# High and low parts side by side: one weight load for 512 columns in the FFN and short-convolution layers of a two-block float32 kernel

## The reference, cut to what matters

```python
def conv_ffn(h, w_up, w_conv, b_conv, w_down):          # twice; D_FF = 2816
    u = h @ w_up                                        # 1024 -> 2 * 2816
    u = depthwise_conv3(u, w_conv) + b_conv             # along the sequence
    val, gate = jnp.split(u, 2, axis=-1)
    return (jax.nn.silu(gate) * val) @ w_down           # 2816 -> 1024

def shortconv_mixer(h, w_in, conv_w, w_out):            # once; WIDTH = 1536
    u = jnp.einsum('bsd,dc->bsc', h, w_in)              # 1024 -> 4 * 1536
    bg, cg, xv, gate = split into four
    y = bg * causal_depthwise_conv(cg * xv, conv_w)
    return jnp.einsum('bsc,cd->bsd', y * jax.nn.silu(gate), w_out)
```

## Time and profile before

| | |
|---|---|
| time, median of 3 runs | 920.02 us (919.19 to 920.58) |
| the profiled execution's own time | 921.24 us |
| its span | 919.5 us |
| mean granted TensorE clock | 0.985 |
| TensorE busy | 881.4 us (96%) |
| VectorE busy | 630.4 us (69%) |
| ScalarE busy | 504.2 us (55%) |
| bytes read from HBM | 151.14 MB, 166 GB/s over the span |

### The profile page before, as it was taken

One profiled execution on the slowest core, in us unless ns is written; L12 is line 12 of the kernel. 1 busy time (PEld: TensorE's weight loads), 2 busy tenths in 40 slices (PEclk: granted clock), 3 DMA queues, 4 the chain that ended last, 5 costly groups with the idle time before them and its releaser, 6 DMA issues.

```text
span 919.5 us, 15132 instructions
## 1 busy us (share of the span) xinstructions
PE 881.4 (96%) x5832; PEld 806.4 (88%) x5832; DVE 630.4 (69%) x848; ACT 504.2 (55%) x676; POOL 34.3 (4%) x76
## 2 busy tenths in 40 slices
PE   7999989999999998899999999999999899999996
PEld 7977769999999876678999999979999699999995
DVE  6798757777666678766776766757877665554643
ACT  6754545455555463545645545558988664353431
POOL 2000100000000023101000000000000000000001
PEclk9999999999999999799999999999999999999998
DMA  9453632745445424054464454516353035545521
GB/s 340 148 200 127 223 137 96 269 143 225 183 149 220 179 95 180 0 185 166 179 240 169 186 205 157 211 65 229 135 231 139 23 138 207 213 162 197 171 81 46
DMA packets 22443, 152.80 MB, mean 166 GB/s; under 512 B 2528, under 2 KB 2656, under 8 KB 5120
## 3 DMA queue, kind: packets, MB, share of 16 engines
q1 hardware_dynamic: 22032, 149.71, 44.1%
q0 software_dynamic: 368, 2.49, 0.7%
HBM read 151.14 MB, written 1.05 MB: 166 GB/s over the span
## 4 chain that ended last, share of the span: by engine, by line
PE 81%; DVE 7%; ACT 5%; issue 1%; POOL 1%; POOLq 0%; ACTq 0%; DVEq 0%
PE ring L1335 47%; PE acc L1348 24%; PE ring L1313 2%; DVE w_lo L761 2%; PE acc L1515 1%; PE ring L1600 1%; PE acc L1280 1%; PE ring L1319 1%; PE ring L1551 1%; ACT xn L457 1%; PE acc L1575 1%; ACT w_hi L448 1%; DVE x L814 0%; ACT pm L647 0%; DVE cacc L1018 0%
## 5 line engine op out<-in xcount | busy, mean ns | idle before, releaser
L761 DVE TENSOR_TENSOR w_lo<-raw,w_hi 128x2048 fp32r<-128x2048 f32 (+1 forms) x146 | 317.8, 2199 | 101.1 <-ACT w_hi L448 100.9
L1335 PE MATMUL ring<-h_hi,w_hi 128*128 128x256 f32 x1264 | 358.6, 284 | 0.0
L1335 PE MATMUL ring<-h_hi,w_lo 128*128 128x256 f32 x1264 | 357.7, 283 | 0.0
L1335 PE MATMUL ring<-h_lo,w_hi 128*128 128x256 f32 x1264 | 357.6, 283 | 0.0
L448 ACT ACTIVATE w_hi<-raw 128x2048 fp32r<-128x2048 f32 (+1 forms) x146 | 264.3, 1839 | 25.4 <-DMA raw<-in_stream_dram 21.8
L1335 PEld LDWEIGHTS ring<-h_lo,w_hi 128*128 128x128 f32 x1264 | 240.7, 190 | 1.5
L1335 PEld LDWEIGHTS ring<-h_hi,w_hi 128*128 128x128 f32 x1264 | 240.7, 190 | 1.4
L1335 PEld LDWEIGHTS ring<-h_hi,w_lo 128*128 128x128 f32 x1264 | 240.7, 190 | 0.0
L1018 DVE SCALAR_TENSOR_TENSOR cacc<-ring,par,cacc 128x255 f32<-128x255 f32 x176 | 76.8, 478 | 52.2 <-ACT cacc L575 47.1
L1348 PE MATMUL acc<-w_hi,a_hi 128*128 128x512 f32 x272 | 107.7, 396 | 3.9 <-DVE a_lo L1195 2.6
L1348 PE MATMUL acc<-w_hi,a_lo 128*128 128x512 f32 x272 | 107.6, 396 | 0.0
(11 more groups left out here) (211 smaller groups left out, 890.8 us busy)
## 6 DMA issues: line engine op xcount, KB each, us to landing
raw<-in_stream_dram SPq DMA_DIRECT2D x134, 1024.0 KB, 4.8
raw<-in_stream_dram SPq DMA_DIRECT2D x12, 512.0 KB, 5.0
gatew<-in_gatew_dram POOLq DMA_DIRECT2D x1, 1536.0 KB, 6.8
x<-in_x_dram SPq DMA_DIRECT2D x2, 512.0 KB, 3.8
out_dram<-xn SPq DMA_DIRECT2D x2, 512.0 KB, 2.6
row<-in_row_dram POOLq DMA_DIRECT2D x1, 640.0 KB, 9.7
gup_raw<-in_gup_dram SPq DMA_DIRECT2D x3, 128.0 KB, 7.0
par<-in_par_dram SPq DMA_DIRECT2D x1, 274.0 KB, 4.5
```

What stands on the lines that cost most here:

```text
L761: nc.vector.tensor_tensor(w_lo[:, u % RING, 0:n], raw[:, u % RAW, 0:n], w_hi[:, u % RING, 0:n].bitcast(f32), ALU.subtract).then_inc(lo_spl ...
L1335: last = nc.tensor.matmul(ring[:, b, f * S:(f + 1) * S], w_parts[a][:, slot, lo:lo + P], h_parts[c][:, kc, :], start=kc == 0 and n == 0, s ...
```

## The change

`h_hi` and `h_lo` become two views of one tile `hh`, high and low side by side for each kc, so that `hh[:, kc, :, :]` is 512 columns. A new function `merged` computes an up unit: for each f and kc one product of `w_hi` by the 512 columns and one of `w_lo` by the 256 high columns, 32 products with 32 loads in place of 48 with 48. The high-by-high and low-by-high sum stands in the left half of a bank, the high-by-low sum in the right half, so a unit now takes two banks (k = 0: banks 0 and 1, k = 1: banks 2 and 3). ACT copies the right halves into a new tile `usum` (`crossed`), DVE adds the left halves to it (`summing`), and all that read the bank before now reads `usum`. TensorE waits for `summed` in place of `ring_free`.

The first unit of each layer goes through `first_merged` (48 products of 256 columns as before, but into two banks), and the last up unit of each of the three layers stays with `wide`, in bank 2 alone, without `usum`. The splits of coming units stand elsewhere in the steps of ACT and DVE.

```diff
-        h_hi = put("h_hi", [P, KC, S], f32r)
-        h_lo = put("h_lo", [P, KC, S], f32r)
+        hh = put("hh", [P, KC, 2, S], f32r)
+        h_hi, h_lo = hh[:, :, 0, :], hh[:, :, 1, :]
...
+            def crossed(units, k):
+
+                act.wait_ge(used, units)
+                nc.scalar.activation(usum[:, k, :, :], ring[:, 2 * k:2 * k + 2, S:2 * S], ACT.Copy).then_inc(cross_ready, 1)
...
-                def taps(e, i, k):
-
-                    act.wait_ge(used, up_unit(B, e, k) + 1 + 6 * i)
+                B, C, J, M = U_FFN[n], C_FFN[n], STEP_FFN[n], SUM_FFN[n]
+
+                def taps(e, i, k, alone=False):
+
+                    if alone:
+                        act.wait_ge(used, up_unit(B, e, k) + 1)
+                    else:
+                        act.wait_ge(summed, M + 2 * e + k + 1 + 4 * i)
                     for half in range(2):
                         c = C + 8 * (2 * e + k) + 4 * half + 32 * i
-                        last = nc.scalar.activation(cacc[:, k, half, :], ring[:, (G + 2 * e + k) % 4, half * S:(half + 1) * S],
+                        last = nc.scalar.activation(cacc[:, k, half, :], ring[:, 2, half * S:(half + 1) * S] if alone else usum[:, k, half, :],
                                                     ACT.Identity, scale=par[:, bass.ds(c + 1, 1)], bias=par[:, bass.ds(c + 3, 1)])
                     last.then_inc(taps_ready, 1)
                 def step(e, i=0, last=False):
+                    crossed(up_unit(B, e, 0) + 1 + 6 * i, 0)
+                    split(B + 5 + 3 * e, i)
                     taps(e, i, 0)
-                    split(B + 5 + 3 * e, i)
-                    taps(e, i, 1)
-                    act.wait_ge(ring_free, G + 2 * e + 2 + 4 * i)
+                    if not last:
+                        crossed(up_unit(B, e, 1) + 1 + 6 * i, 1)
+                        split(B + 6 + 3 * e, i)
+                    taps(e, i, 1, alone=last)
+                    act.wait_ge(ffn_conv, 2 * J + 2 * e + 2 + 4 * i)
                     nc.scalar.activation(sgl[:, :, :], cacc[:, :, 1, :], ACT.Silu).then_inc(gate_ready, 1)
                     act.wait_ge(act_ready, J + e + 1 + 2 * i)
                     act.wait_ge(used, B + 3 * e - 1 + 6 * i)
                     nc.scalar.activation(a_hi[:, e % 2, :, :], actf[:, :, :], ACT.Copy).then_inc(a_hi_ready, 1)
                     if not last:
-                        split(B + 6 + 3 * e, i)
                         split(B + 7 + 3 * e, i)
...
-                act.wait_ge(used, up_unit(U_SC, e, 0) + 1 + 6 * i)
-                nc.scalar.activation(cgs[:, :], ring[:, (GEN["sc"] + 2 * e) % 4, 0:S], ACT.Copy).then_inc(cg_ready, 1)
-                act.wait_ge(used, up_unit(U_SC, e, 1) + 1 + 6 * i)
-                nc.scalar.activation(sgs[:, :], ring[:, (GEN["sc"] + 2 * e + 1) % 4, S:2 * S], ACT.Silu).then_inc(gate_ready, 1)
-                for k in range(splits):
-                    if k == 1:
-                        ahead(e, i)
-                    split(U_SC + 5 + 3 * e + k, i, half=sc_half(U_SC + 5 + 3 * e + k))
-                if splits < 2:
-                    ahead(e, i)
+                c = C_SCONV + 3 * e + 6 * i
+                crossed(up_unit(U_SC, e, 0) + 1 + 6 * i, 0)
+                if splits:
+                    split(U_SC + 5 + 3 * e, i, half=sc_half(U_SC + 5 + 3 * e))
+                act.wait_ge(pp_ready, e + 1 + 2 * i)
+                nc.scalar.activation(ct[:, :], pp[:, :], ACT.Identity, scale=par[:, bass.ds(c + 2, 1)], bias=0.0).then_inc(taps_ready, 1)
+                if splits:
+                    crossed(up_unit(U_SC, e, 1) + 1 + 6 * i, 1)
+                    act.wait_ge(summed, SUM_SC + 2 * e + 2 + 4 * i)
+                    gate = usum[:, 1, 1, :]
+                else:
+                    act.wait_ge(used, up_unit(U_SC, e, 1) + 1)
+                    gate = ring[:, 2, S:2 * S]
+                nc.scalar.activation(sgs[:, :], gate, ACT.Silu).then_inc(gate_ready, 1)
                 act.wait_ge(act_ready, STEP_SC + e + 1 + 2 * i)
                 act.wait_ge(used, U_SC + 3 * e - 1 + 6 * i)
                 nc.scalar.activation(a_hi[:, e % 2, 0, :], acts[:, :], ACT.Copy).then_inc(a_hi_ready, 1)
-
-            def ahead(e, i):
-
-                c = C_SCONV + 3 * e + 6 * i
-                act.wait_ge(ring_free, GEN["sc"] + 2 * e + 1 + 4 * i)
-                nc.scalar.activation(ct[:, :], pp[:, :], ACT.Identity, scale=par[:, bass.ds(c + 2, 1)], bias=0.0).then_inc(taps_ready, 1)
+                for k in range(1, splits):
+                    split(U_SC + 5 + 3 * e + k, i, half=sc_half(U_SC + 5 + 3 * e + k))
...
+            def summing(units, k):
+
+                dve.wait_ge(cross_ready, units)
+                nc.vector.tensor_tensor(usum[:, k, :, :], ring[:, 2 * k:2 * k + 2, 0:S], usum[:, k, :, :],
+                                        ALU.add).then_inc(summed, 1)
...
                 def step(e, i=0, last=False):
+                    summing(M + 2 * e + 1 + 4 * i, 0)
+                    split(B + 4 + 3 * e, i)
                     conv(e, i, 0)
-                    split(B + 5 + 3 * e, i)
-                    conv(e, i, 1)
+                    if last:
+                        conv(e, i, 1, alone=True)
+                    else:
+                        summing(M + 2 * e + 2 + 4 * i, 1)
+                        split(B + 5 + 3 * e, i)
+                        conv(e, i, 1)
+                        split(B + 6 + 3 * e, i)
                     dve.wait_ge(gate_ready, J + e + 1 + 2 * i)
                     own.wait()
                     nc.vector.tensor_tensor(actf[:, :, :], cacc[:, :, 0, :], sgl[:, :, :], ALU.mult).then_inc(act_ready, 1)
                     dve.wait_ge(a_hi_ready, J + e + 1 + 2 * i)
                     nc.vector.tensor_tensor(a_lo[:, e % 2, :, :], actf[:, :, :], a_hi[:, e % 2, :, :].bitcast(f32),
                                             ALU.subtract).then_inc(a_lo_ready, 1)
-                    if not last:
-                        split(B + 6 + 3 * e, i)
-                        split(B + 7 + 3 * e, i)
+                    if last:
+                        split(B + 5 + 3 * e, i)
...
                 c = C_SCONV + 3 * e + 6 * i
+                summing(SUM_SC + 2 * e + 1 + 4 * i, 0)
+                dve.wait_ge(summed, SUM_SC + 2 * e + 1 + 4 * i)
+                nc.vector.tensor_tensor(pp[:, :], usum[:, 0, 0, :], usum[:, 0, 1, :], ALU.mult).then_inc(pp_ready, 1)
+                if splits:
+                    split(U_SC + 4 + 3 * e, i, half=sc_half(U_SC + 4 + 3 * e))
                 dve.wait_ge(taps_ready, 2 * STEP_LRU + LRU_ITERS + e + 1 + 2 * i)
                 own.mark(nc.vector.scalar_tensor_tensor(out=ct[:, 1:S], in0=pp[:, 0:S - 1], scalar=par[:, bass.ds(c + 1, 1)],
                                                         in1=ct[:, 1:S], op0=ALU.mult, op1=ALU.add))
                 own.wait()
                 own.mark(nc.vector.scalar_tensor_tensor(out=ct[:, 2:S], in0=pp[:, 0:S - 2], scalar=par[:, bass.ds(c, 1)],
                                                         in1=ct[:, 2:S], op0=ALU.mult, op1=ALU.add))
+                if splits:
+                    summing(SUM_SC + 2 * e + 2 + 4 * i, 1)
+                    dve.wait_ge(summed, SUM_SC + 2 * e + 2 + 4 * i)
+                    branch = usum[:, 1, 0, :]
+                else:
+                    dve.wait_ge(gate_ready, STEP_SC + e + 1)
+                    branch = ring[:, 2, 0:S]
                 own.wait()
+                own.mark(nc.vector.tensor_tensor(ys[:, :], branch, ct[:, :], ALU.mult))
                 dve.wait_ge(gate_ready, STEP_SC + e + 1 + 2 * i)
-                nc.vector.tensor_tensor(ys[:, :], ring[:, (g + 1) % 4, 0:S], ct[:, :], ALU.mult).then_inc(ring_free, 1)
-                dve.wait_ge(ring_free, g + 2 + 4 * i)
+                own.wait()
                 nc.vector.tensor_tensor(acts[:, :], ys[:, :], sgs[:, :], ALU.mult).then_inc(act_ready, 1)
+                if splits:
+                    split(U_SC + 5 + 3 * e, i, half=sc_half(U_SC + 5 + 3 * e))
+                dve.wait_ge(a_hi_ready, STEP_SC + e + 1 + 2 * i)
+                nc.vector.tensor_tensor(a_lo[:, e % 2, 0, :], acts[:, :], a_hi[:, e % 2, 0, :].bitcast(f32),
+                                        ALU.subtract).then_inc(a_lo_ready, 1)
+                if splits == 3:
+                    split(U_SC + 6 + 3 * e, i, half=sc_half(U_SC + 6 + 3 * e))
...
+            def merged(u, k, i=0, done=None):
+
+                ready(u, i)
+                if done is not None:
+                    pe.wait_ge(summed, done)
+                for f in range(2):
+                    for kc in range(KC):
+                        lo = kc * 256 + f * P
+                        nc.tensor.matmul(ring[:, 2 * k + f, :], w_hi[:, u % RING, lo:lo + P], hh[:, kc, :, :],
+                                         start=kc == 0, stop=False, skip_group_check=True)
```

(19 more changed lines are left out.)

71 lines of the change are left out of this document (37 added, 34 removed).

## The result

The change takes 911.28 us (median of 4 runs, 910.53 to 912.32) where before takes 920.03. The ratio is 0.9908 (95% interval 0.9895 to 0.9920): 8.5 us gained. I had forecast 12.6 us. The range ended at 911.3: the median lies on that end, and by the ratio (911.6 for 920.02) the time lies just past it. The sign and what was said of waits in this kernel held; the size of the main term did not.

A forecast was written before the change was run, and what follows sets the result against it. TensorE bounds the kernel, time in the changed layers being products times start distance. Merging's 11.4 us plus SC's tail, 1.16, make 12.6 us off the 920.02 median: 907.4 us, range 904.9 to 911.3.

The forecast's parts named there:

- The sign: Whole kernel: faster by over 0.2% at 95%, no measurable change 2%, slower 3%.
- the main term: Merged up units of the FFNs and SC: 992 triples saving 0.0115 us each, 11.4 us gained.
- The bound, the counts, the mechanism: FFNs and SC: time is products times start distance; 62 merged units, 992 triples, each losing one start and one load.
- The step that failed: In `merged`, three products of 0.360 us become one of 512 and one of 256 columns, 0.349 us together.
- The forecast case: Whole kernel: likeliest case, 78%, 905.3 to 909.7 us, from gains of 13.4 and 10.7 us with half a microsecond each way.
- the seams: Layer boundaries: rival, 10%, half-clock stretches cost up to 1.7 us each, a late `w_lo` a microsecond; 909.7 to 912 us.
- The rule of the Trainium skill: Merged triples: distance is columns/2.4 plus 2.5 ns, so 2.5 us saved; nearly-free-start rival, 7%, gives 916.4 us.
- The tail of SC: SC's last step: `ct` and taps need only the first up unit, so the last down unit's wait goes, 1.16 us.
- The cover: FFNs and SC: added `crossed`, `summing` and moved splits lie beside TensorE, which stands far behind their results; cost nothing.
- the 6.9 us of slack: Each FFN: if ACT and DVE bound the step, 6.9 us of lag is absorbed before TensorE loses time.
- It turns the sign from a step of 17.9 us on: FFNs: rival, 3%, ACT and DVE become the bound; at 18.6 us a step 936 us, slower than before from 17.9.
- the split ahead of `residual`: End of an FFN: DVE's 2.29 us split behind the last `a_lo` costs nothing, 0.5 us if its cover were gone.

The follow-up runs named there:

- experiment 1: The change with each merged triple again as three products of 256 columns, banks, sums and moved splits kept: 919.07 us, ratio 0.9983 to the kernel before.
- Experiment 3: The change with each half of a merged unit issuing eight 512-column products, then eight of 256: 908.02 us, ratio 0.9867 to the kernel before.
- heavier: The change with the first `w_lo` of each FFN step computed twice on VectorE, 2.29 us more: 940.02 us, ratio 1.0219 to the kernel before.

## Why the prediction was wrong, point by point

**The bound, the counts, the mechanism: right.** TensorE's distances are the time of these layers, before and after; 992 triples lost a start and a load each, and experiment 1 puts 6.9 of the 8.5 us on that.

**The step that failed:** "In `merged` three products (0.360 us) become one of 512 and one of 256 columns: 0.229 + 0.120 = 0.349". Each summand was right where it was measured, in rows of products of one size. The sum was not: the change alternates the sizes one by one, and then a pair takes 352.8 ns. The term came to 6.9 us instead of 11.4. I had taken bounds for a product of 512 columns, and none for the order; the order costs 3.7 to 5 ns a pair, 4 to 5 us in all. Experiment 3 shows it: only the order changed, the distances are 0.229 and 0.120 again, and the ratio of 0.9867 is 907.8 us of 920.03, where I had said 907.4. The range had an error of its own besides. The forecast case's 905.3 to 909.7 does not follow from its bounds, which with the tail and half a microsecond each way give 905.0 to 908.7; that 911.3 was all but reached is owed to the room left for lost clock at the seams, which is not what happened.

**The rule of the Trainium skill** (TensorE: Matmul & The Clock Gate, Back-to-back issue gap), which the page gives for products taken singly and by which a start saved is worth 2.5 ns: the trace does not agree. A start saved, with its load, is worth 7 ns alternating and 11 to 12 in runs. Nor does the rule have any term for what stands next to a product.

**The tail of SC:** right, 1.16 us forecast, 1.4 and 1.5 us in the two kernels that have it alone, with intervals of a microsecond each way, and the wait gone from the rows.

**The cover:** the claim that sums and splits cost nothing held, by rows (idle 0.0) and by experiment 1. What I said of the case without it did not: the 6.9 us of slack are not to be subtracted, so "It turns the sign from a step of 17.9 us on" was too generous (`heavier` has a step of 17.52 us and is 2.2% slower than before).

**The seams:** the split ahead of `residual` cost nothing. The stretches at half clock differ between single executions, longer in the attention and one fewer behind FFN 1 and ahead of SC in the change's; experiment 1, which has the same seams and was timed twelve times, leaves no room for a loss of a microsecond.

**What stays open:** why products of 512 and 256 columns that alternate one by one stand further apart than in pairs. In the change's rows the starts of the 512-column products stand 0.36, 0.35 and 0.35 us apart in turn, over and over (285.17, 285.53, 285.88, 286.23, 286.59): the loss comes in every third pair, and the two others have the 0.35 of the forecast. Bank, half of the bank, the side that streams, and the alternation between `w_hi` and `w_lo` are excluded by runs. A fixed price for each change of size is excluded too. Against products in runs without an end (0.2266 + 0.120, 346.6 ns a pair) a change of size and back costs some 6 ns alternating, 4 in runs of two, and 18 to 20 in runs of eight or sixteen. Not varied in any run are the weight loads: each product has one of its own throughout.

## What to carry to other kernels

Two distances read in rows of like products may not be added for a mixed sequence; find a row of the mixture, or give the order a bound of its own, and issue equal sizes at least in pairs, which cost nothing here. A chain behind the last unit of a layer is worth keeping short even at the price of a costlier product there: the instructions added to it showed in full in the FFNs, and by half in SC. And slack between engines in the middle of a layer is no gain that may be subtracted: it may be missing at the layer's start, and at its end the last consumer waits for whatever lag has gathered.
